# Modulation of a hybrid recurrent block in eight pieces, summed beside the first head pair's projections

## What is computed

```python
s_lat, s_ctx = silu(c), silu(c_ctx)
m_lat = split(s_lat @ w_ada + b_ada, 6)          # w_ada: 2048 x 12288
m_ctx = split(s_ctx @ w_ada + b_ada, 6)
a_lat = rms_norm(x,   norm_mix) * (1 + m_lat[1]) + m_lat[0]
a_ctx = rms_norm(ctx, norm_mix) * (1 + m_ctx[1]) + m_ctx[0]
q, v, g = split(a @ w_in, 3);  z = clip(a @ w_f[dir], -30, 30)
log_f = log_sigmoid(z) + log1p(lb * exp(-z));  k = (1 - lb) * sigmoid(-z)
o = chunked scan of both directions;  y = (rms_norm(o) * silu(g)) @ w_o
h = x + m_lat[2] * y
h = h + m_lat[5] * swiglu(rms_norm(h) * (1 + m_lat[4]) + m_lat[3])
```

## Time and profile before

| | |
|---|---|
| median of 3 runs | 1825.56 us (1825.11 to 1826.02) |
| profiled execution, time | 1824.11 us |
| its span | 1822.3 us |
| TensorE (PE) busy | 1774.7 us, 97% |
| VectorE (DVE) busy | 1263.6 us, 69% |
| ScalarE (ACT) busy | 899.5 us, 49% |
| DMA | 353.82 MB, mean 194 GB/s |
| mean granted clock of TensorE | 0.996 |

### The profile page before, as it was taken

The page is one execution under the profiler, slowest core; times in us unless marked ns, Lnnn a source line. Parts: engine busy times, 40 slices in busy tenths (PEclk is TensorE's granted clock), DMA queues, the critical chain, the costliest instruction groups (busy, mean ns, idle before and its releaser), DMA issues.

```text
span 1822.3 us, 25084 instructions
## 1 busy us (share of the span) xinstructions
PE 1774.7 (97%) x9791; PEld 1496.8 (82%) x9791; DVE 1263.6 (69%) x1977; ACT 899.5 (49%) x1279; POOL 0.2 (0%) x4
## 2 busy tenths in 40 slices
PE   7999999999999999999889989999999999999997
PEld 2268989898989898988789878888888888888886
DVE  6753879796979797978985575555555555555755
ACT  6762635354545454545446554444444444444554
POOL 0000000000000000000000000000000000000000
PEclk9999999999999999999999999999999999999998
DMA  9954645554544554445667557777777777655553
GB/s 381 409 199 139 196 128 156 155 175 124 156 132 137 170 174 129 141 148 150 205 195 262 186 152 216 221 237 224 224 216 238 222 222 230 217 196 194 192 193 127
DMA packets 178136, 353.82 MB, mean 194 GB/s; under 512 B 16929, under 2 KB 82786, under 8 KB 176994
## 3 DMA queue, kind: packets, MB, share of 16 engines
q1 hardware_dynamic: 177826, 352.18, 60.4%
q10 hardware_dynamic: 192, 0.05, 0.0%
HBM read 350.06 MB, written 2.11 MB: 193 GB/s over the span
## 4 chain that ended last, share of the span: by engine, by line
PE 85%; DVE 9%; ACT 2%; issue 2%; DMA 1%; SPq 0%; ACTq 0%; DVEq 0%
PE bank L1431 9%; PE bank L1433 9%; PE bank L1432 9%; PE bank L1307 8%; PE bank L1308 8%; PE bank L1309 8%; PE bank L1322 3%; PE bank L1323 3%; PE bank L1324 3%; PE bank L1451 3%; PE bank L1453 3%; PE bank L1452 3%; PE score L1511 2%; DVE rawlo L818 2%; PE score L1451 1%
## 5 line engine op out<-in xcount | busy, mean ns | idle before, releaser
L818 DVE TENSOR_TENSOR rawlo<-raw,whi 128x1024 fp32r<-128x1024 f32 x496 | 605.6, 1224 | 434.1 <-ACT whi L495 433.2
L495 ACT ACTIVATE whi<-raw 128x1024 fp32r<-128x1024 f32 x496 | 522.6, 1058 | 656.2 <-PE bank L1433 240.3
L1307 PE MATMUL bank<-ahi,whi 128*128 128x256 f32 (+1 forms) x1024 | 352.1, 344 | 10.8 <-DVE rawlo L818 10.6
L1308 PE MATMUL bank<-alo,whi 128*128 128x256 f32 (+1 forms) x1024 | 344.4, 336 | 0.0
L1309 PE MATMUL bank<-ahi,rawlo 128*128 128x256 f32 (+1 forms) x1024 | 344.4, 336 | 0.0
L1431 PE MATMUL bank<-whi,ahi 128*128 128x512 f32 x704 | 275.9, 392 | 1.8 <-DVE alo L1149 1.8
L1433 PE MATMUL bank<-whi,alo 128*128 128x512 f32 x704 | 274.5, 390 | 0.0
L1432 PE MATMUL bank<-rawlo,ahi 128*128 128x512 f32 x704 | 274.5, 390 | 0.0
L1307 PEld LDWEIGHTS bank<-ahi,whi 128*128 128x128 f32 x1024 | 194.4, 190 | 32.2 <-DVE rawlo L818 10.3
L1309 PEld LDWEIGHTS bank<-ahi,rawlo 128*128 128x128 f32 x1024 | 194.3, 190 | 20.2
L1308 PEld LDWEIGHTS bank<-alo,whi 128*128 128x128 f32 x1024 | 194.6, 190 | 19.0
(11 more groups left out here) (226 smaller groups left out, 2279.3 us busy)
## 6 DMA issues: line engine op xcount, KB each, us to landing
raw<-in_w_ada_dram SPq DMA_DIRECT2D x168, 512.0 KB, 4.3
raw<-in_ffn_w_gate_dram SPq DMA_DIRECT2D x88, 512.0 KB, 3.7
raw<-in_ffn_w_up_dram SPq DMA_DIRECT2D x88, 512.0 KB, 3.7
raw<-in_ffn_w_down_dram SPq DMA_DIRECT2D x88, 512.0 KB, 4.3
raw<-in_hg_w_in_dram SPq DMA_DIRECT2D x128, 256.0 KB, 3.7
raw<-in_hg_w_f_dram SPq DMA_DIRECT2D x128, 256.0 KB, 3.7
raw<-in_hg_w_in_dram SPq DMA_DIRECT2D x32, 512.0 KB, 4.8
raw<-in_hg_w_o_dram SPq DMA_DIRECT2D x32, 512.0 KB, 4.3
```

What stands on the lines that cost most here:

```text
L495: act.activation(whi[:, ck % SPL, :], raw[:, q % RAW, :], ACT.Copy).then_inc(s_hi, 1)
L818: dve.tensor_tensor(low(ck), raw[:, SEQ["w", ck] % RAW, :], whi[:, ck % SPL, :].bitcast(F32), ALU.subtract).then_inc(s_lo, 1)
L1307: pe.matmul(dst, w, ah, start=start, stop=False, skip_group_check=True)
L1308: pe.matmul(dst, w, al, start=False, stop=False, skip_group_check=True)
```

## The change

The 4096 columns are summed in eight pieces instead of four quarters. Piece e holds shift and scale of k-tiles 2e and 2e + 1 (256 + 256 columns). It has eight blocks, each of two rows of k: 2 x 2 x 256 columns, 512 KB, in two transfers. Six blocks (0, 1, 3, 5, 10, 11) are direct, 58 are split. High parts go to three slots made of `zt` and `aacc` (`mhi`), low parts over the raw block. Chunks of pair 0 are ordered VQ, Z, VQ, Z, and twelve blocks stand ahead of chunk 0; then four beside each of the chunks 0 to 12. Piece e + 1 is turned and applied while the chunks of the k-tiles before run. Pair 0's gates get banks of their own (`score`, `ob`, bank 3), so values and queries stay in banks 0 to 2 up to chunk 15. The small rows are loaded ahead of x, x ahead of all blocks, and the x transposes, the roots and their matmul stand before block 0. The constants `keep` and `masks` are loaded at chunk 14 instead of 4, and the other factors begin at chunk 14 instead of 9.

```diff
+MRAW = 6
+MHI = 3
+FIRST = 12
+C_B = 0
+def mod_direct(n):
+    return n in (0, 1, 3, 5, 10, 11)
+def mod_blocks(ck):
+    return list(range(FIRST + 4 * ck, min(FIRST + 4 * ck + 4, 64)))
...
+            if g == 0 and p < 16:
+                yield C_B + p, ("VQ", "Z")[p % 2], 0, p // 2, tasks
...
+            def load_mod(n):
+                if n >= MRAW:
+                    sp.wait_ge(s_du, n - MRAW + 1)
+                e, j = divmod(n, 8)
+                for m in range(2):
+                    sp.dma_start(dslot[n % MRAW][:, m * 512:(m + 1) * 512].rearrange("p (k n) -> p k n", k=2),
+                                 wmod[:, 2 * j:2 * j + 2, m * D + e * 256:m * D + (e + 1) * 256]).then_inc(s_dir[n % MRAW], 16)
...
+                if ck == 1:
+                    for n in range(8, FIRST):
+                        load_mod(n)
+                elif ck >= 2:
+                    for n in mod_blocks(ck - 2):
+                        load_mod(n)
                 load(ck)
...
+            def mod_hi(n):
+                if mod_direct(n):
+                    return
+                j = SPLIT_MOD.index(n)
+                act.wait_ge(s_dir[n % MRAW], 32 * (n // MRAW + 1))
+                if j >= MHI:
+                    act.wait_ge(s_du, SPLIT_MOD[j - MHI] + 1)
...
+                act.activation(mhi[j % MHI][:, :], dslot[n % MRAW], ACT.Copy).then_inc(s_mh, 1)
...
+                if u == 0 and kind == "VQ":
+                    for n in mod_blocks(ck):
+                        mod_hi(n)
+                if u == 0 and kind == "Z" and r < 7:
+                    for n in mod_blocks(ck)[:3]:
+                        mod_hi(n)
+                    modulate(2 * r + 2)
+                    modulate(2 * r + 3)
+                    for n in mod_blocks(ck)[3:]:
+                        mod_hi(n)
+                hi(ck + 1)
+                if u == 0 and kind == "VQ" and r < 7:
+                    mod_rows(r + 1)
+                if kind == "Z" and r == (0 if u else 7):
                     values(u)
...
+                    if u == 0 and i < 2:                       # chunk_vq, after bank group i
+                        for n in mod_blocks(ck)[2 * i:2 * i + 2]:
+                            mod_block(pe, n)
+                    if u == 0 and i == 4 and r < 7:
+                        turn_rows(pe, r + 1)
...
+                    if u == 0 and i >= 3:                      # chunk_z
+                        for n in mod_blocks(ck)[i - 3:i - 2]:
+                            mod_block(pe, n)
...
-    begin = ADA_ENDS[e - 1] + 1 if e else KD // 2 + 1
+    begin = ADA_ENDS[e - 1] + 1 if e else 14
```

More of the change, by code:

```diff
@@ L182, in build @@
                  + [arena[:, 4 * D + 2 * P + i * CW:4 * D + 2 * P + (i + 1) * CW] for i in range(3)])
+        dlow = ([over(f"dlow{i}", "work", KD * TT + i * CW, [P, CW]) for i in range(3)]
+                + [over(f"dlow{i + 3}", "arena", 4 * D + 2 * P + i * CW, [P, CW]) for i in range(3)])
+        mhi = [over("mhi0", "zt", 2 * TT, [P, CW]), over("mhi1", "aacc", 0, [P, CW]), over("mhi2", "zt", 0, [P, CW])]
         ident = sb("ident", [P, P])
@@ L684, in _ @@
                     gate_sigmoid((ck - C_B) // 16 - 1, p - 2)
-                if kind == "Z" and r == 0:
+                if kind == "Z" and r == (0 if u else 7):
                     queries(u)
@@ L900, in ada @@
+            mod_lo(8)
+            mod_lo(9)
+            modulation(0)
+            dve.wait_ge(s_lb, 4)
+            dve.tensor_tensor(lbv, lbt[:, 0, :], lbt[:, 0, :], ALU.subtract).then_inc(s_lb, 1)
+            a_lo(0)
+            a_lo(1)
+            x_norm(4)
+            x_norm(5)
+            dve.wait_ge(s_lb, 5)
+            dve.tensor_scalar(oml[:, :], lbv, -1.0, 1.0, ALU.mult, ALU.add).then_inc(s_mod, 1)
             def ada(i):
@@ L1078, in _ @@
             for ck, kind, u, r, tasks in positions():
-                if ck > C_B + KD // 2:
-                    lo(ck + 1)
+                if u == 0 and kind == "VQ":
+                    for n in mod_blocks(ck):
+                        mod_lo(n)
+                    if r < 5:
+                        x_norm(6 + 2 * r)
+                        x_norm(7 + 2 * r)
+                if u == 0 and kind == "Z" and r < 7:
+                    for n in mod_blocks(ck)[:3]:
+                        mod_lo(n)
+                    modulation(r + 1)
+                    a_lo(2 * r + 2)
+                    a_lo(2 * r + 3)
+                    for n in mod_blocks(ck)[3:]:
+                        mod_lo(n)
+                lo(ck + 1)
                 p = (ck - C_B) % 16
@@ new lines, in mod_block @@
+            for k in range(2):
+                first, end = j == 0 and k == 0, j == 7 and k == 1
+                if mod_direct(n):
+                    last = pe.matmul(mod_bank(e)[0:4, :], csd[:, 2 * j + k, :, :].rearrange("p i s -> p (i s)"),
+                                     w[:, :, k, :], start=first, stop=end, skip_group_check=True)
+                else:
+                    cc = cs4[:, 2 * j + k, :, :].rearrange("p i s -> p (i s)")
+                    pe.matmul(mod_bank(e)[0:4, :], cc, wh[:, :, k, :], start=first, stop=False, skip_group_check=True)
+                    last = pe.matmul(mod_bank(e)[0:4, :], cc, wl[:, :, k, :], start=False, stop=end, skip_group_check=True)
@@ L1314, in v_bank @@
                 first, end = k == 0, k == KD - 1
-                if first and u:
+                if first and u == 1:
+                    pe.wait_ge(s_vev, half + 1)
+                elif first and u:
                     pe.wait_ge(s_zc, 4 * (u - 1) + 1 + 2 * half)
```

352 lines of the change are left out of this document (151 added, 201 removed).

## The result

| | before | after |
|---|---|---|
| median of the runs compared | 1825.34 us (1824.39 to 1826.02, 4 runs) | 1815.13 us (1814.67 to 1817.04, 4 runs) |
| profiled execution, its span | 1824.11, 1822.3 us | 1817.04, 1815.3 us |
| first matmul of pair 0's projection | 108.67 us | 45.95 us |
| first matmul of pair 1 | 187.81 us | 181.55 us |
| mean granted clock | 0.996 | 0.994 |

The account below looks back on a forecast made before the run. Bound: modulation filled DMA while no projection could run, then pair 0 filled TensorE. 40.6 + 21.4 + 94.4 + 8.8 + 6.0 + 9.8 put pair 1 at 181.0, 6.8 us earlier: 1818.8 us, 8-in-10 range 1813 to 1827.

Parts of the forecast that it names:

- chunks 0 and 1: First two chunks of pair 0: TensorE waits 2.3, 0.3 for next blocks, 1.0 in chunk 1; 21.4 us together.
- a pair of chunks, 2 to 11: Five alike pairs: 17.8 us of TensorE work, waits 0.9 at the Z chunk's fourth block and 0.2 in VQ; 18.9 each.
- Up to chunk 0: Kernel start: x tiles, spread roots at 19.3, their matmul, then twelve blocks with the queue full; chunk 0 starts at 40.6 us.
- rival 4: TensorE's gaps behind the x transposes: lower clock, 4 us if four blocks ran so; part of case 2, no own chance.
- case 2: No change that can be told: at 1.85 us per 512 KB pair 1 starts at 185.6, time 1823.4; chance 0.13.
- Transfers: Block loads with 1 KB runs: 1.76 to 1.50 us for 512 KB, taken as 1.64 us.
- Rival 3: Queue between 40 and 160 us: transfers decide from 277 GB/s down; at 250 GB/s 14.1 us more, 1839.7; chance 0.15.
- The one-by-one case: 80 loads at 3.6 us each, without overlap, behind x: pair 1 near 303 us, 115 us later; chance 0.01.
- Rival 1: From chunk 0 on no waits, 512 KB in 1.50 us: 17.3 us less, 1808.3; chance 0.10 for over 10 less.
- The sum: Whole kernel: pair 1 starts at 181.0 instead of 187.8, 6.8 us less, forecast 1818.8 us.
- Edits at nothing: Later copies of pair 0's values and queries, and later sums of the other factors, were to cost nothing; up to 1 us otherwise.
- What moves the start of pair 1 moves the end by as much: Behind pair 0: TensorE waits only 1.2 us from 188 to 700 us, so the end shifts with that start.

Follow-up runs that it names:

- serial_pieces: The changed kernel with all 64 blocks ahead of chunk 0 and the pieces' sums in two banks by turns: 1880.1 us, ratio 1.0285 to the kernel before.
- change_repeated: The changed kernel run again with nothing edited, for a third trace: median 1817.77 us, ratio 0.9952 to the kernel before.
- quarter_transfers: The changed kernel with each block in four transfers of 128 KB instead of two of 256 KB: 1821.02 us, ratio 0.9972 to the kernel before.
- serial_five_slots: serial_pieces with five places for high parts instead of three: 1881.61 us, ratio 1.0302 to the kernel before.

## Why the prediction was right, and where its terms were off

The seam that moves, the sign and the start of pair 1 came out as forecast; the terms in between less so. Of the two things that the forecast counted on, TensorE's smaller work is the one that shows as time (10.4 us less ahead of pair 1). That the DMA engines and TensorE now work side by side left TensorE 4.2 us more of idle time than before, but it is what hides the splits: serial_pieces, without it, is 53 us slower than the kernel before.

| step | forecast | after |
|---|---|---|
| 512 KB with 1 KB runs, queue full | 1.64 us | 1.50 us (349 GB/s) |
| chunk 0 starts | 40.6 | 45.95 |
| chunks 0 and 1 | 21.4 | 19.8 |
| a pair of chunks, 2 to 11 | 18.9 | 18.34 |
| chunk 12, chunk 13 | 8.8, 6.0 | 8.7, 5.6 |
| chunks 14 and 15 | 9.8 | 9.9 |
| pair 1 starts | 181.0 | 181.55 |

**Up to chunk 0: 5.3 us too early.** The last spread root, forecast at 19.3, was there at 18.5, but I let the matmul over them follow at once. It also waits for VectorE's sixteenth copy, whose bank it writes, and the copies began late because the small rows came late: block 0 was used at 25.5 instead of 22.5. The queue then stood still, which I had ruled out with "so the queue stays full". Of rival 4 the size was right. From 38.6 to 42.4 us two split blocks and the transposes ran at half pace, about 1.9 us lost; the roots' matmul and block 0 some 1.7 more (they took 4.4 us, and 2.75 in change_repeated, where the clock stayed up). But I had given it only a part of case 2 and kept it out of the sum.

**Transfers: my fast bound was the price.** With the queue full, 1 KB runs gave 347 to 349 GB/s at a share of 1.10 to 1.11, the 1.50 us that I had as the lower end. Rival 3, transfers as the bound from 277 GB/s down, had room: from 66 to 158 us the share was 0.89 at 286 GB/s, which is what ten loads of 512 KB in a pair of 18.34 us ask for. The condition that the rival named, 277 GB/s or less, did not come. In quarter_transfers, with 286 GB/s offered for a while, chunks 0 and 1 took 20.7 us instead of 18.5 to 19.9, and of the five later pairs one grew, by 1.35 us. The one-by-one case is far off: a transfer of 256 KB took 5.2 us from issue to landing, and one landed every 0.75 us, so about seven were in flight:

```profile
work<-in_w_ada_dram SPq DMA_DIRECT2D x66, 256.0 KB, 5.2
```

**Chunks 0 and 1, 1.6 us too long; a pair of chunks, 0.5 too long.** Both terms held waits that did not come. In chunks 0 and 1 I had 3.6 us of waits and 17.8 of work; it was 1.4 and 18.4. This error and that of the start are linked in part: in the three traces of the change chunk 0 began at 44.62, 45.95 and 47.58, and the two chunks took 19.9, 19.8 and 18.5 us. For the fourth block I had counted 0.9 us behind `modulate` and 0.2 more in the VQ chunk; from 66 to 158 us TensorE waited 1.4 us in all, 0.28 a pair. Its own work was 18.06 instead of my 17.8. So the term was 0.82 too long for waits and 0.26 too short for work. Rival 1 (pairs with no waits, 17.8) was nearer for the pairs, but the late start, which it did not have, ate that.

**The sum.** The errors are +5.35 for the start, -1.6 for chunks 0 and 1, -2.7 for the five pairs and -0.5 for chunks 12 to 15; together +0.55. The right total is made of errors that cancel: that is luck, and only the start of each chunk shows it.

**Edits at nothing.** They cost nothing: TensorE's waits behind 188 us are the same row as before.

**From pair 1 to the end.** "What moves the start of pair 1 moves the end by as much" holds over the traces here: from 175 to 244 us the start moved, and what lay behind stayed within 1633.8 to 1637.2. The 3.4 us by which the median fell further than forecast are not in any trace; the two repeats gave a gain of 9.7 and 8.4.

## What to carry to other kernels

Work that fills the DMA engines and work that fills TensorE belong side by side, but what this is worth is read from TensorE's own work once it sets the pace. The gain here needed both halves. With the overlap and 25 direct blocks the kernel is 8.7 us slower than before; with six direct blocks and no overlap it is 53 us slower. Side by side the splits hide, so blocks can be moved from the expensive direct form to the cheap split one, and that is what shortened the time. When such a start is forecast, follow every in-order engine from the first instruction: a small row that lands late ahead of a large tile, and a bank shared by two steps, decided when the ring of six places began to turn. Judge a change of a few microseconds by a marker inside the trace (here the first matmul of pair 1) and by several executions, since the rest of the kernel varies by 3 us by itself.

## What the runs showed of the hardware

- **Issuing is a rate of its own.** A transfer costs the issuing queue about 0.47 us, at 128 and at 256 KB. At 128 KB that is 281 GB/s, below the 349 that the DMA engines moved with a full queue.
- **Shorter runs cost bandwidth, not dramatically.** 1 KB runs moved 347 to 349 GB/s at a share of 1.10 to 1.11, 4 KB runs 408 at 1.02.
- **TensorE's clock fell in more places than I had thought.** Behind waits of 1.8 and 2.4 us the granted clock was 0.50 (1.2 GHz) over a full stretch of 2 us, but in change_repeated it stayed up behind the same wait of 1.83 us; in serial_five_slots, with TensorE busy 13 of 20 us, it averaged 0.66 to 0.74; near 880 to 930 us it fell in one execution and not in the next at the same place. The Trainium skill, "TensorE: Matmul & The Clock Gate", section "What's actually happening", has the same two levels; the traces agree, with starts 0.43 us apart at the one and 0.23 at the other.
